# Gathering the other expert rows during the last item, with one-hot products for the last item's rows

## The reference

```python
logits = (t @ router).astype(jnp.float32)          # t: 512 x 1024
top_v, top_i = lax.top_k(logits, 2)
gates = jax.nn.softmax(top_v, axis=-1)
comb = jnp.sum(jax.nn.one_hot(top_i, 8) * gates[..., None], axis=1)
out = jnp.zeros_like(t)
for e in range(8):
    out = out + comb[:, e:e+1] * ((silu(t @ wg[e]) * (t @ wu[e])) @ wd[e])
x = x + g_f * rms_norm(out, post_ffn_g[l])
```

## Time and profile before

| | us |
|---|---|
| runs | 1463.5, 1463.55, 1457.72 |
| median | 1463.5 |
| profiled execution, its own time | 1458.68 |
| its span, first to last instruction | 1457.1 |
| last product of the last item starts | 1422.92 |
| first instruction that combines gathered rows on VectorE | 1437.18 |

### The profile page before, as it was taken

How to read it: one execution, slowest core, us unless ns; L and a number is a source line. 1 busy time by engine, 2 the same in 40 slices (tenths; PEclk the granted TensorE clock), 3 DMA queues, 4 the chain that set the end, 5 groups by cost and what they waited for, 6 DMA issues and landing times.

```text
span 1457.1 us, 16745 instructions
## 1 busy us (share of the span) xinstructions
PE 1309.0 (90%) x5901; PEld 1041.5 (71%) x5901; DVE 938.3 (64%) x1315; ACT 709.3 (49%) x1068; POOL 117.8 (8%) x158
## 2 busy tenths in 40 slices
PE   1897989799999999997988997899999999999990
PEld 1775447688888788876774474778887878788880
DVE  5956781665565457457476516686687668667885
ACT  4444441632122132136345514485687568657884
POOL 1370060000000000003300000200000000000002
PEclk9999999999999999998999998899999999999995
DMA  9931332146454464463542000797699679868995
GB/s 337 337 124 32 138 121 72 60 131 212 149 183 164 145 217 154 157 218 85 222 168 82 6 29 0 289 385 268 229 306 351 209 237 365 280 218 287 371 385 187
DMA packets 142632, 288.05 MB, mean 198 GB/s; under 512 B 6974, under 2 KB 48492, under 8 KB 142572
## 3 DMA queue, kind: packets, MB, share of 16 engines
q1 hardware_dynamic: 132172, 252.39, 49.9%
q0 software_dynamic: 10256, 34.87, 6.7%
q10 hardware_dynamic: 144, 0.00, 0.0%
HBM read 266.01 MB, written 21.23 MB: 197 GB/s over the span
## 4 chain that ended last, share of the span: by engine, by line
PE 78%; DVE 10%; ACT 5%; issue 4%; DMA 2%; ACTq 0%; POOL 0%; SPq 0%; DVEq 0%; POOLq 0%
PE ps L602 19%; PE ps L604 19%; PE ps L603 19%; PE ps L614 3%; PE ps L956 3%; PE ps L955 3%; DVE acc L1452 3%; PE ps L764 2%; PE ps L783 2%; PE ps L743 2%; ACT spl L1293 1%; PE ps L752 1%; DVE spl L1849 1%; DMA x<-in_x 1%; DMA mraw<-in_moe_w_down 1%
## 5 line engine op out<-in xcount | busy, mean ns | idle before, releaser
L1849 DVE TENSOR_TENSOR spl<-mraw,spl 128x1024 fp32r<-128x1024 f32 (+2 forms) x288 | 311.5, 1130 | 86.4 <-ACT spl L1293 85.5
L1293 ACT ACTIVATE spl<-mraw 128x1024 fp32r<-128x1024 f32 (+2 forms) x288 | 266.3, 979 | 118.1 <-PE ps L956 91.4
L1093 ACT ACTIVATE spl<-raw 128x2048 fp32r<-128x2048 f32 (+2 forms) x56 | 100.7, 1799 | 233.1 <-PE ps L604 194.9
L602 PE MATMUL ps<-hT,spl 128*128 128x512 f32 x416 | 164.7, 396 | 8.1 <-DVE hT L1513 8.1
L1436 DVE TENSOR_TENSOR spl<-raw,spl 128x2048 fp32r<-128x2048 f32 (+2 forms) x56 | 120.7, 2158 | 74.7 <-ACT spl L1093 74.1
L603 PE MATMUL ps<-hT,spl 128*128 128x512 f32 x416 | 163.4, 393 | 0.0
L604 PE MATMUL ps<-hT,spl 128*128 128x512 f32 x416 | 163.4, 393 | 0.0
L602 PE MATMUL ps<-spl,xgT 128*128 128x512 f32 (+1 forms) x384 | 147.1, 383 | 14.7 <-DVE spl L1849 11.8
L604 PE MATMUL ps<-spl,xgT 128*128 128x512 f32 (+1 forms) x384 | 144.4, 376 | 0.0
L603 PE MATMUL ps<-spl,xgT 128*128 128x512 f32 (+1 forms) x384 | 144.3, 376 | 0.0
L1452 DVE SCALAR_TENSOR_TENSOR acc<-raw,cond,acc 128x512 f32<-128x512 f32 x154 | 118.7, 771 | 5.4
(11 more groups left out here) (323 smaller groups left out, 2311.4 us busy)
## 6 DMA issues: line engine op xcount, KB each, us to landing
raw<-in_w_mod SPq DMA_DIRECT2D x48, 1024.0 KB, 6.0
mraw<-in_moe_w_down SPq DMA_DIRECT2D x40, 1024.0 KB, 7.8
mraw<-in_moe_w_gate SPq DMA_DIRECT2D x34, 1024.0 KB, 6.6
mraw<-in_moe_w_up SPq DMA_DIRECT2D x34, 1024.0 KB, 6.7
mraw<-in_moe_w_gate SPq DMA_DIRECT2D x16, 768.0 KB, 6.5
mraw<-in_moe_w_up SPq DMA_DIRECT2D x16, 768.0 KB, 7.8
raw<-in_ffn_w_gate SPq DMA_DIRECT2D x11, 1024.0 KB, 8.2
raw<-in_ffn_w_up SPq DMA_DIRECT2D x11, 1024.0 KB, 5.2
```

The lines of the kernel that those rows point to most:

```text
L602: mm(o, lh, rh, start=start, stop=False)
L1093: A(spl[:, s % SPLS, 0, 0:n], raw[:, r % RAWS, 0:n], ACT.Copy).then_inc(hi_ready, 1)
L1293: A(spl[:, (SB + j) % SPLS, 0, c], mraw[:, j % MRAWS, c], ACT.Copy).then_inc(half_ready, 1)
L1849: ins = V.tensor_tensor(o[:, 1, c], mraw[:, j % MRAWS, c], o[:, 0, c].bitcast(F32), ALU.subtract)
```

## The change

- GpSimd's item loop ends one item earlier (`n1 = n - 1`). In the last item GpSimd loads the item's gates and the next (unused) rows, then gathers all 512 tokens' first rows into four tiles `yt`, waits for all four DMAs, and gathers the second rows onto them with DMAs that add (`compute_op: ALU.add`). Row numbers that lie in the last item are replaced by a row of zeros.
- The last item's result is not written back. VectorE builds 0/1 matrices `pickl` (which row of the item belongs to which token) ahead of the items. After the last item TensorE transposes them, VectorE copies them out of PSUM, and TensorE multiplies them with `ye` (plain float32, 8 products of 128x512).
- The gates go into a DRAM buffer `gates` in the order of `scratch` by 8 indirect DMAs of 128 single numbers. In each item GpSimd loads 128 of them, and ScalarE applies them as it copies `ye` out of PSUM; for the second tile of a pair VectorE multiplies after its addition.
- The combination at the end is one addition of PSUM and `yt`, instead of a product on ScalarE and a product with an addition on VectorE.

```diff
@@ gpsimd
+            g.dma_start(gates_dram.rearrange("(p c) o -> p (c o)", p=P), gp[:, 1, 0:SCRATCH_TILES + 3]).then_inc(
+                zero_dma, 16)
...
+            eng.wait_ge(slots_ready, 2)
+            for t in range(T):
+                for k in range(2):
+                    g.indirect_dma_start(out=gates_dram[0:SCRATCH_TILES * P, :], out_offset=bass.IndirectOffsetOnAxis(
+                        ap=sli[:, k, t:t + 1], axis=0), in_=gt[:, k, t:t + 1], in_offset=None).then_inc(scat_dma, 16)
+            eng.wait_ge(scat_dma, 16 * 4 * T)
...
+            n1 = eng.value_load(eti[0:1, 3:4], min_val=3, max_val=MAXI - 1)
...
                 for b in range(2 if pair else 1):
+                    g.dma_start(place_gate[b][0:height(b), :], gates_dram[bass.ds(row + P * b, height(b)), :]).then_inc(
+                        gate_dma[b], 16)
...
-            with eng.Fori(n4, n) as k:
+            with eng.Fori(n4, n1) as k:
                 item(k, False, k * P + n2 * HP, k * P + n2 * HP + P, False, None)
-            for t in range(T):
-                for k in range(2):
-                    g.indirect_dma_start(out=yg[:, t, k, :], ...).then_inc(yg_dma[t], 16)
+            eng.wait_ge(xg_ps[0], n)
+            g.dma_start(place_gate[0][:], gates_dram[bass.ds(n * P + n2 * HP - P, P), :]).then_inc(gate_dma[0], 16)
+            eng.wait_ge(last_ready, 1)
+            g.dma_start(xg[0][:], scratch[0:P, :]).then_inc(xg_dma[0], 16)
+            for k in range(2):
+                if k:
+                    eng.wait_ge(yg_dma, 16 * T)
+                for t in range(T):
+                    g.indirect_dma_start(out=yt[t][:], out_offset=None, in_=scratch,
+                                         in_offset=bass.IndirectOffsetOnAxis(ap=slg[:, k, t:t + 1], axis=0),
+                                         **({"compute_op": ALU.add} if k else {})).then_inc(yg_dma, 16)
@@ tensor, after the items
+                eng.wait_ge(last_ready, 2)
+                eng.wait_ge(xg_full[0], n + 1)
+                for t in range(T):
+                    last = tr(ps[:, 2, P * t:P * t + P], pickl[:, t, :])
+                last.then_inc(pickT_ps, 1)
+                eng.wait_ge(pickT_ready, 1)
+                eng.wait_ge(ye_ev[0], n)
+                for t in range(T):
+                    for h in range(2):
+                        last = mm(ps[:, 2 * t + h, :], pickT[:, P * t:P * t + P], ye[0][:, 512 * h:512 * h + 512],
+                                  start=True, stop=True)
+                    last.then_inc(last_ps, 1)
@@ scalar
+                    eng.wait_ge(gate_dma[0], i * 16 + 16)
+                    A(ye[0][:].rearrange("p (h c) -> p h c", h=2), ps[:, 4:6, :], ACT.Copy,
+                      scale=place_gate[0][:, 0:1]).then_inc(ye_ev[0], 1)
@@ vector, ahead of the item loop (two more row-number steps and four more picks follow)
+                V.tensor_scalar(slgf[:], slf[:], last0[:, 1:2], float(ZERO_ROW), ALU.is_ge, ALU.mult)
+                link(V.tensor_scalar(rel[:], slf[:], last0[:, 1:2], None, ALU.subtract))
+                for t in range(T):
+                    ins = V.tensor_scalar(pickl[:, t, :], row_of[:], rel[:, 0, t:t + 1], None, ALU.is_equal)
...
@@ vector, end of a pair
+                        V.tensor_scalar(ye[1][0:HP, :], ye[1][0:HP, :], place_gate[1][0:HP, 0:1], None,
+                                        ALU.mult).then_inc(ye_ev[1], 1)
@@ vector, after the items
+                eng.wait_ge(pickT_ps, 1)
+                V.tensor_copy(pickT[:], ps[:, 2, :]).then_inc(pickT_ready, 1)
...
-                        after(V.scalar_tensor_tensor(out=ym[:, t, :], in0=yg[:, t, 1, :], ...), ym_ready, t + 1)
+                        eng.wait_ge(yg_dma, 32 * T)
+                        eng.wait_ge(last_ps, t + 1)
+                        after(V.tensor_tensor(y, ps[:, 2 * t:2 * t + 2, :], y, ALU.add), ym_ready, t + 1)
```

More of the change, by code:

```diff
@@ L47 @@
 RAWS, SPLS, MRAWS = 4, 3, 6
-MAXT = 16
-MAXI, MAX2, MAXF = 15, 7, 11
+MAXT = 18
+MAXI, MAX2 = 16, 7
 HP = P // 2
@@ L176, in build @@
         xfull = at("xfull", W_ + 53760, [P, KD, P])
-        ym = at("ym", W_ + 18944, [P, T, D])
+        yt = [at(f"yt{t}", o, [P, D]) for t, o in enumerate((W_ + 42496, W_ + 46592, W_ + 27136, HT_ + 24576))]
+        zt = [at(f"zt{b}", W_ + 18944 * b, [P, D]) for b in range(2)]
+        junk = at("junk", W_ + 4096, [P, D])
         small = [W_ + 12288]
@@ L211, in build @@
         owner = little("owner", [P, 2, MAXT])
-        etf = little("etf", [P, 3 + 2 * MAXT])
-        eti = little("eti", [P, 3 + 2 * MAXT], I32)
+        etf = little("etf", [P, 4 + 2 * MAXT])
+        eti = little("eti", [P, 4 + 2 * MAXT], I32)
+        last0 = little("last0", [P, 2])
+        rel = little("rel", [P, 2, T])
+        slg = little("slg", [P, 2, T], I32)
+        slgf = little("slgf", [P, 2, T])
+        place_gate = [little(f"place_gate{b}", [P, 1]) for b in range(2)]
         assert small[0] <= W_ + 18944
@@ L306, in build @@
             "e_silu", "e_mul", "aT_ps", "aT_hi", "aT_ready", "ye_ev", "ye_dma"))
-        yg_dma = [sem(f"yg_dma{t}") for t in range(T)]
+        yg_dma = sem("yg_dma")
         gate_low, gate_sum, up_low, up_sum, ye_low = map(sem, ("gate_low", "gate_sum", "up_low", "up_sum", "ye_low"))
@@ L568, in item @@
                 for b in range(2 if pair else 1):
-                    eng.wait_ge(scat_dma, 16 * 2 * T)
+                    eng.wait_ge(scat_dma, 16 * 4 * T)
+                    g.dma_start(place_gate[b][0:height(b), :], gates_dram[bass.ds(row + P * b, height(b)), :]).then_inc(
+                        gate_dma[b], 16)
+                for b in range(2 if pair else 1):
+                    eng.wait_ge(scat_dma, 16 * 4 * T)
                     eng.wait_ge(*((ye_ev[0], i + 1) if b == 0 else (ye_ev[1], pairs_done)))
@@ L1377, in experts @@
                     item(k, None, None)
[L1379 to L1385, removed]
+                for t in range(T):
+                    eng.wait_ge(ym_ready, t + 1)
+                    post_stat(3, t, yt[t][:], junk[:])
             eng.dma_start(cond[:, 0, :], a["c"][0].rearrange("(p k) -> p k", k=KD)).then_inc(c_dma, 16)
@@ L1934, in experts @@
                 n, n2, n4 = counts(eng)
+                link(V.tensor_scalar(last0[:, 0:1], etf[:, 1:2], float(HP), -float(P), ALU.mult, ALU.add))
+                link(V.scalar_tensor_tensor(out=last0[:, 1:2], in0=etf[:, 0:1], scalar=float(P), in1=last0[:, 0:1],
+                                            op0=ALU.mult, op1=ALU.add))
+                V.tensor_scalar(slgf[:], slf[:], last0[:, 1:2], float(ZERO_ROW), ALU.is_ge, ALU.mult)
+                link(V.tensor_scalar(rel[:], slf[:], last0[:, 1:2], None, ALU.subtract))
+                for t in range(T):
+                    ins = V.tensor_scalar(pickl[:, t, :], row_of[:], rel[:, 0, t:t + 1], None, ALU.is_equal)
+                link(V.tensor_tensor(slgf[:], slgf[:], slf[:], ALU.max))
+                V.tensor_copy(slg[:], slgf[:]).then_inc(last_ready, 1)
+                for t in range(T):
+                    ins = V.scalar_tensor_tensor(out=pickl[:, t, :], in0=row_of[:], scalar=rel[:, 1, t:t + 1],
+                                                 in1=pickl[:, t, :], op0=ALU.is_equal, op1=ALU.add)
+                ins.then_inc(last_ready, 1)
                 with eng.Fori(0, n2) as i:
```

58 lines of the change are left out of this document (30 added, 28 removed).

## The result

The changed kernel takes 1475.0 us (median of five runs, 1471.84 to 1477.39), the kernel before 1461.63 on the same chip (five runs). The ratio is 1.0094, with a 95% interval of 1.0074 to 1.0115: slower by 13.4 us, outside the range of the prediction (1453 to 1471) and on the side to which it gave 0.25. The profiled execution took 1475.71, its span is 1474.1, against 1457.1. In the tables, one of the four runs of a4 was slow, 1969.3; the median of its three fast ones is 1484.54, and all ratios go by fast runs alone.

What follows compares the result with a forecast made beforehand. The prediction took TensorE as the bound, with DMA right behind it in item 7. Terms -8.4 + 5.9 + 0.9 + 0.4 + 2.0 = +0.8 us gave 1464.3 at the median; it named 1463, range 1453 to 1471.

Steps and rivals of the forecast that it cites:

- The end: Stretch after the last item's products: write-back, landing, gathers and ScalarE's first product go, 8.4 us gained.
- E: The point where TensorE ends the last item's last product; VectorE's first addition was forecast at 6.9 after it, before 13.9.
- The bound of 10.1: Most that the end could gain, if TensorE's last products run at full clock; the sum took 8.4.
- Item 7: Last item: gathers share full DMA engines with the weights, so 5.9 us are lost to waits, bounds 0 to 10.4.
- the plain price: In item 7, an adding gather was counted as costing what a plain one does; two reads would add 5.2 us.
- 4.5 that are borne: In item 7, weights may land 4.5 us late without loss, set against 10.4 us of gathers.
- rival (a): In item 7, adding gathers cost two reads: 11.1 us lost, sum +6.0, 1469.5 at the median; chance 0.30.
- Item 0: First item: VectorE's new steps and the gate scatters together lose 2.0 us, bounds 0 to 6.
- VectorE's 1.4: At the start of item 0, VectorE's new steps take 3.1 us, 1.7 of it free, 1.4 on the path.
- Pairs and scale: VectorE's gate product after the third pair loses 0.9 us; the scale on ScalarE's evictions loses 0.4.
- (b): Gathers are hidden: item 7 loses 0 to 1, 1453.5 to 1457 at the median; chance 0.20.
- (c): At the end, VectorE waits for late second gathers, so nothing is gained there, time over +8; chance 0.05.

Runs made afterwards that it cites:

- a4: Changed kernel with all eight gathers held back until the last item's result has left PSUM: 1486.59 us, ratio 1.0174 to the kernel before.
- a2: Changed kernel with the result buffer released before the gate scatters are issued and awaited: 1479.59 us, ratio 1.0135 to the kernel before.
- a3: Changed kernel with the second four gathers overwriting instead of adding: 1469.19 us, ratio 1.0053 to the kernel before.
- a5: Changed kernel with no adds and twelve plain gathers, four then eight at once, four of them into unread tiles: 1477.91 us, ratio 1.0110 to the kernel before.
- a6: Changed kernel with each gate scattered as a row of 512 bytes instead of 4 bytes: 1471.35 us, ratio 1.0070 to the kernel before.
- v2: As v1, but all eight gathers at once at the start of item 7 and unused units loaded in full: 1467.41 us, ratio 1.0045.
- a1: Changed kernel without the eight scatters of single gate numbers: 1466.22 us, ratio 1.0039 to the kernel before.
- b1: Kernel before with only the eight scatters of 4-byte gate numbers added, read by nobody: 1473.15 us, ratio 1.0075.
- v3: v1 with the result buffer released before GpSimd builds the matrices: 1464.38 us, ratio 1.0023 to the kernel before.
- v1: Changed kernel with gates in one-hot and diagonal matrices instead of DRAM, plain gathers, second four delayed, unused loads shrunk: 1466.15 us, ratio 1.0028.
- v4: v3 with GpSimd's 13 building operations moved into the pair items: 1456.28 us, ratio 0.9955 to the kernel before.

## Why the prediction was wrong

The sum was -8.4 + 5.9 + 0.9 + 0.4 + 2.0 = +0.8. In the same terms the profiles have -10.3 + 11.4 + 1.0 + 0.5 + 10.2 = +12.8.

**The end, right, and better by 1.9.** Write-back and landing are gone and VectorE is late with its split and copy, as worked out. VectorE's copy began at 1452.97, E + 1.9 and not E + 2.5, and I took the lower clock after an idle of 2.7, where the products ran at the full one after an idle of 1.83. The bound of 10.1 that I named for full clock was the value, and that was luck: the idle alone does not settle the clock. In a2, a3 and a5 it was 3.05 and the 16 records took 8.73 to 8.83, in a4 they did so after 2.74; but in a6 they took 7.13 after 3.05. The products in a6 and a3:

```profile
1448.86 7.13 PE L1087 MATMUL ps<-ye,pickT 128*128 128x512 f32 x16 [3.05 <-DVE pickT L2008]
...
1453.21 8.73 PE L1085 MATMUL ps<-ye,pickT 128*128 128x512 f32 x16 [3.05 <-DVE pickT L2004]
```

The end was 1.5 to 2.1 longer than in the changed kernel in a2, a3 and a5, and 0.5 in a6.

**Item 7: the term that was mis-sized is "I take the plain price in the sum".** The step beside it held for this order of gathers: without the addition the loss is 6.4 (a3), where 5.9 was worked out from 10.4 of the engines less 4.5 that are borne. The same bytes cost 8.3 all at once (v2), so the 4.5 is no fixed slack, and the close match is in part luck. The addition costs as much as a second plain gather (a5, and the queue's share for each MB), 5.0 more. That is rival (a) in mechanism and in size, 11.4 against its 11.1. I gave it 0.30, because no row showed such a transfer; but the page that I cited then stated the price, and of all that I had it was the only evidence on it. The Trainium skill, Collectives: The Full Stack, section "The bandwidth ceiling: the fold count and why AG ≠ RS ≠ AR", says that an add in the DMA engine needs two source reads: these runs agree in the price, for a gather too (49.9% against 25.1% for each MB), though no view shows a read by itself.

**Item 0: the step that failed is the price of the gate scatters.** I bounded them by 5.9 from packets of the earlier trace rows, and set them against landings that were slow already, so that 2.0 remained with VectorE's 1.4. VectorE's part was about right (1.6 in a1), though TensorE's idle before the third unit came to 2.14, and 2.42 in a1, instead of the 3 named as a sign. The scatters cost 8.7 (a1) to 10.1 (b1), and though profiles of like kernels differ by 3 or 4 us in this stage, the medians moved by 8.8 and 10.0 too. It is not through their own packets, which are a quarter as many as I took (256, not 1024) and cheaper (3.9% of 160 for 167, 0.037 each, against 0.092), but by what they do to the weights' packets beside them. With 256 packets my bound would have been 1.5. The earlier trace rows had small packets, yet none showed a write of 4 bytes with weights in flight; I took a price for a bound. The wait for the buffer behind all 16 scatters was not in the prediction, though it is GpSimd's next instruction; by a2 and v3 its removal alone gains nothing.

**Pairs and scale, right.** After the third pair TensorE waits for 1.30 instead of 0.25, in the timeline of the changed kernel; item 6 is 1.0 longer, where 0.9 was worked out, and it is 48.4 again in v1 to v4, where VectorE has no product behind the pair:

```profile
1349.11 0.50 PE L635 MATMUL ps<-spl,xgT 128*128 128x512 f32 x1 [1.30 <-DVE spl L1894]
```

The eviction with a gate takes 1.10 instead of 1.00, and the five items before lose 0.5 in all, 0.06 to 0.13 each, against 0.4 for the scale.

**The rivals.** (b), hidden gathers, is out: with plain ones the loss is 6.4, and only v1, v3 and v4, which send the second four behind the last weights needed, come near to it (1.6 to 2.5). (c) is out: VectorE never waits for `yt`. What my cases lacked is that two of them can hold at once: (a) alone gave 1469.5 at the median, and with 8 more in item 0 it passes the range. I had written that it might, and still ended the range at 1471.

**What stays open.** How writes of 4 bytes slow other queues' packets is not shown, only that 512-byte writes don't. What sets the clock of the last products is open. How v1's 6.2 less in item 7 than v2's divides between the delay and the smaller loads is open too.

## What to carry to other kernels

Beside the share of the DMA engines read the GB/s: a full share at half the bytes is a transfer that costs more than its size, and it is paid by whoever shares the engines. Before a small per-row value is scattered to DRAM or an addition put into a transfer, look for idle time of a compute engine to do it: here a diagonal product on TensorE and steps on GpSimd, placed in a loop turn in which nobody waits for it, kept the gain of 9 at the end and lost 2.5. A transfer moved into a full stretch is to be priced by its bytes less the slack of the waiting engine, and the slack by where it stands: the same eight plain gathers cost 6.4, 8.3 and, with half of them behind the last load that is needed and smaller unused loads, 1.6 to 2.5.

## What the hardware showed that was not expected

- 1024 writes of 4 bytes by indirect DMA, 256 packets in the trace, cost 8.7 to 10.1 us beside weight loads (a1, b1), while the software queue shows 3.9%; weights' packets of about 2 KB took 0.175 us instead of 0.074, and one issue on GpSimd 7.03 us instead of 0.96. With 512 bytes each they cost 0.3 in item 0 (56.83 against 56.57).
- An indirect gather that adds occupies the engines twice as long for each MB: 49.9% against 25.1% of a stretch of 10 us.
- GpSimd's 128x128 operations with two scalars took from 0.79 to 3.62 us each in v1; what made the long ones long is not shown.
- After an idle of 1.83 TensorE's one-hot products ran at the full clock (16 records in 7.13). After 3.05 the same 16 took 8.73 in a3 and 7.13 in a6: an idle time of equal length left the clock at either level.
